# Two of 18 weight slots handed over at step 2 instead of step 4, and the later steps' order of work from step 2 on

## What is computed

```python
x = x + pool_mixer(rms_norm(x, norm_mix), pool_w, pool_scale)
h = rms_norm(x, norm_ffn)
# router: best of 4 groups, best 2 of its 8 experts, gates
for e in range(32):          # rows h[tokens of e]
    g, u = split(h_e @ w_gu[e])        # 1024 -> 2 x 512
    y_e = (silu(g) * u) @ w_dn[e]      # 512 -> 1024
x = x + sum over a token's two experts of gate * y_e
out = rms_norm(x, norm_final)
```

## Time and profile before

| | |
|---|---|
| median of 3 runs | 662.24 us (662.08 to 662.79) |
| the profiled execution | 663.27 us, of which the span is 661.5 us |
| PE, PE weight loads, DVE, ACT, POOL busy | 94%, 80%, 92%, 81%, 24% of the span |
| moved by DMA | 242.83 MB, mean 367 GB/s |
| PE's mean granted clock | 0.983 of full speed |

### The profile page before, as it was taken

One profiled execution on the slowest core, in us unless ns is written; L12 is line 12 of the kernel. 1 busy time (PEld: TensorE's weight loads), 2 busy tenths in 40 slices (PEclk: granted clock), 3 DMA queues, 4 the chain that ended last, 5 costly groups with the idle time before them and its releaser, 6 DMA issues.

```text
span 661.5 us, 9555 instructions
## 1 busy us (share of the span) xinstructions
PE 622.6 (94%) x3460; PEld 526.4 (80%) x3460; DVE 606.2 (92%) x501; ACT 535.7 (81%) x458; POOL 157.9 (24%) x127
## 2 busy tenths in 40 slices
PE   6899989999999999999999999897999989989983
PEld 4799978887888888888888888686877868767872
DVE  5887688989999999999999999897989889998987
ACT  5996626688898989898988988887879688978794
POOL 5000010032222222222222222252225222340311
PEclk9999989999999999999999999999999989989997
DMA  8997769999999999999999999999999999999985
GB/s 293 421 418 278 244 209 374 397 343 302 322 381 404 390 400 393 386 401 374 402 367 401 364 401 366 402 379 392 381 384 386 385 413 384 410 409 400 380 335 211
DMA packets 43637, 242.83 MB, mean 367 GB/s; under 512 B 8184, under 2 KB 9344, under 8 KB 19011
## 3 DMA queue, kind: packets, MB, share of 16 engines
q1 hardware_dynamic: 34322, 220.39, 84.2%
q0 software_dynamic: 9264, 21.79, 12.1%
HBM read 227.19 MB, written 26.21 MB: 383 GB/s over the span
## 4 chain that ended last, share of the span: by engine, by line
DMA 54%; PE 34%; DVE 5%; ACT 3%; issue 2%; SPq 0%; POOL 0%; ACTq 0%; POOLq 0%; DVEq 0%
DMA raw<-in_expert_w_gu 32%; PE psum L1724 19%; DMA raw<-in_expert_w_down 17%; PE psum L1736 3%; PE psum L1652 3%; PE psum L1670 2%; DMA total<-ysb,src_all 2%; PE psum L1638 2%; DMA raw<-total 1%; PE psum L1776 1%; DMA pw_in<-in_pool_w 1%; PE psum L1661 1%; DVE raw L1548 1%; PE psum L1678 1%; PE psum L1787 1%
## 5 line engine op out<-in xcount | busy, mean ns | idle before, releaser
L1210 DVE TENSOR_TENSOR w_lo<-raw,w_hi 128x2048 fp32r<-128x2048 f32 x113 | 255.4, 2284 | 7.8 <-ACT w_hi L884 7.4
L884 ACT ACTIVATE w_hi<-raw 128x2048 fp32r<-128x2048 f32 x113 | 213.5, 1914 | 21.8 <-DMA raw<-in_expert_w_gu 12.8
L1210 DVE TENSOR_TENSOR w_lo<-raw,w_lo 128x2048 fp32r<-128x2048 f32 x79 | 178.5, 2283 | 2.4 <-ACT w_lo L884 2.3
L884 ACT ACTIVATE w_lo<-raw 128x2048 fp32r<-128x2048 f32 x79 | 149.5, 1914 | 13.2 <-DMA raw<-in_expert_w_gu 10.2
L710 POOL DMA_INDIRECT total<-ysb,src_all x28 | 53.5, 1910 | 338.5 <-ACT ysb L979 323.9
L1724 PE MATMUL psum<-w_lo,x_hi 128*128 128x512 f32 x432 | 127.1, 397 | 5.8 <-DVE x_lo L1446 5.8
L1724 PE MATMUL psum<-w_lo,h_hi 128*128 128x512 f32 x376 | 108.3, 395 | 0.5 <-DVE h_lo L1480 0.5
L1724 PEld LDWEIGHTS psum<-w_lo,x_hi 128*128 128x128 f32 x432 | 81.0, 190 | 23.2 <-DVE x_lo L1446 6.7
L696 POOL DMA_INDIRECT xg<-normed,src_all x31 | 78.2, 2523 | 21.5 <-DVE src_all L1305 12.3
L1724 PEld LDWEIGHTS psum<-w_lo,h_hi 128*128 128x128 f32 x376 | 70.9, 190 | 15.5 <-DVE h_lo L1480 0.9
L1736 PE MATMUL psum<-w_lo,x_hi 128*128 128x512 f32 x276 | 74.0, 392 | 0.0
(11 more groups left out here) (208 smaller groups left out, 865.4 us busy)
## 6 DMA issues: line engine op xcount, KB each, us to landing
raw<-in_expert_w_gu SPq DMA_DIRECT2D x128, 1024.0 KB, 10.9
raw<-in_expert_w_down SPq DMA_DIRECT2D x64, 1024.0 KB, 11.8
res<-in_x SPq DMA_DIRECT2D x8, 512.0 KB, 9.7
normed<-nx POOLq DMA_DIRECT2D x8, 512.0 KB, 7.3
total<-res SPq DMA_DIRECT2D x8, 512.0 KB, 8.7
raw<-total SPq DMA_DIRECT2D x8, 512.0 KB, 13.4
out<-raw SPq DMA_DIRECT2D x8, 512.0 KB, 3.9
pw_in<-in_pool_w SPq DMA_DIRECT2D x1, 1024.0 KB, 8.1
```

Of the source, the lines that this page charges most:

```text
L884: nc.scalar.activation(hi_at(s0, j), raw[q][:], ACT.Copy).then_inc(hi_done, 1)
L1210: V.tensor_tensor(w_lo[q][:], raw[q][:], hi_at(s0, j).bitcast(f32), ALU.subtract)\
```

## The change

`FREE_STEP` goes from 4 to 2 and `FIRST` with it from 22 to 10: two raw slots become places for upper parts at pair 10, steps 2 and 3 use the later order on ACT and DVE, and two calls are moved so that they still happen in step 2. The slots 16 and 17 are never loaded; load m waits for pair m-16 from load 16 on. From pair 34 to pair 131 all that loads and upper parts wait for is as before.

```diff
-    FREE_STEP = HEAD
-    GIVEN = {HEAD: 2, E - 10: 2}
+    FREE_STEP = 2
+    GIVEN = {FREE_STEP: 2, E - 10: 2}
@@ ACT, step
                 if s < E - 1:
-                    copy_y(gate_all[:, s - 2:s - 1], start(s), s - 2)
+                    gates_of_y(s - 2)
+                    copy_y(gate_now[:] if s == 2 else gate_all[:, s - 2:s - 1], start(s), None if s == 2 else s - 2)
@@ DVE, early_step
                     if s == 1 and j == GU_PAIRS + 1:
                         turned_tables()
-                    if s == 2 and j == 0:
-                        tables_by_step()
@@ DVE, step
                     hidden(s - 1)
                     if s < E:
                         low_x(s, is_small(s))
+                    if s == 2:
+                        tables_by_step()
                 up_to(low_next, low_pair, s, n + 3)
```

## The result

| | before | changed |
|---|---|---|
| median of 12 runs | 662.60 us | 664.23 us |
| ratio, 95% interval | | 1.0019 (1.0011 to 1.0028) |
| the profiled execution, its span | 663.27, 661.5 us | 663.85, 662.1 us |
| PE, DVE, ACT busy | 94%, 92%, 81% | 94%, 91%, 81% |
| moved by DMA | 242.83 MB | 242.83 MB |

The change makes the kernel some 1.3 us slower. That is 0.19%, just inside the 0.2% taken as the bound of "no change", though the interval leaves 1 out. Two timings of one and the same kernel, further down, came out 0.28% apart, so the profiles have to carry the argument.

The account below looks back on a forecast made before the run. Free slots were taken to limit loads until about 220 us, then the DMA engines. Late start +0.8 us (between +1.9 and -0.3, PE's gain) on a median of 662.24 us gave 663.0 us; own range 661.6 to 664.1, overall to 665.3.

Parts of the forecast that it names:

- What bounds the kernel: Weight loads: limited by free slots up to about 220 us, after that by the DMA engines themselves.
- a shift that arises after 270 us: Stated sign of being wrong: the loads' shift arising in the DMA-limited part instead of before it.
- The lag at load 25: Load 25, waiting for pair 9, lands at 137.7 instead of 132.9 us: 4.8 us late.
- The hole behind load 33: Gap of 8 us between issues of loads 33 and 34, DMA partly idle; forecast to disappear.
- What makes the lag good: DMA idle time, 154 to 170 us, absorbs the late start: +1.9 us left by shares, -0.3 by bytes; +0.8 taken.
- The new stall: PE waits about 0.85 us for hid(1) near 129.5 us, as pairs 10 and 11 come first on ACT and DVE.
- The old one: PE's stall before the turn of hid(3) at 165.38 us, worth 1.15 us, was to go.
- The sum on PE: Old stall's 1.15 us less new stall's 0.85 us: PE gains 0.3 us from pair 21 on.
- Pair 130: Loads 142 and 143 wait for pairs two later; nothing expected, since SyncE waits for landings there; uncovered 2.7 us.
- The late start is not made good: Rival: idle share at 154 to 162 us can't be filled; +3.4 us, 665.6 us; chance 0.22.
- No stall: Rival: PE's stall near 129.5 us doesn't show and the stream isn't behind; -1.15 us, 661.1 us; chance 0.09.
- The clock falls: Rival: PE's clock drops to half rate at the stall near 129.5 us; +2.2 us, 664.4 us; chance 0.06.

Follow-up runs that it names:

- e5_wait_14: Kernel before, with loads 16 to 33 also waiting on SyncE for pair m-14, two pairs later than pair m-16; ratio 1.0086.
- e4_step4_head: Kernel before, but at the head of step 4 ACT takes one pair instead of two before silu(3), DVE none before hid(3); ratio 0.9978.
- e1_wait: Kernel before with one SyncE wait added: loads 16 to 33 also wait for pair m-16; compute orders unchanged; ratio 1.0013.
- e9_before_itself: Kernel before, letter for letter, timed against itself with no edit; ratio 0.9993.
- e3_hid_first: Changed kernel, but in step 2 silu(1) and hid(1) come before pairs 10 and 11 on ACT and DVE; ratio to before 0.9999.
- e2: Changed kernel's slots and places, but steps 2 and 3 in the early order, as in the kernel before; ratio to before 1.0019.
- e7: Changed kernel's slots and places with steps 2 and 3 in the early order, a repeat timing of e2; ratio to before 1.0005.
- e8: Kernel before, with loads 142 and 143 waiting for pairs 128 and 129 instead of 126 and 127; ratio 1.0017.
- e10: Same code as e8, timed again: kernel before with loads 142 and 143 waiting for the later pairs; ratio 0.9989.

## Why the prediction was right, point by point

The number fell inside the range and the sign was right, but in part by luck: the lag was made good in full, and then a loss that no term of the sum had brought the time back.

**What bounds the kernel** was right as to who waits for whom. e5_wait_14 moves the end by 0.86% with nothing but SyncE's waits. e4_step4_head lets PE run 1.1 us earlier, and the delay at load 181 is -0.8 us. The rule that I drew from it was wrong: that the end moves by as much as the stream is ahead or behind when it stops waiting for slots, a state "settled between 100 and 220 us". At load 52 the changed kernel is 0.4 us early and e1_wait on time; at load 181 they are 1.4 and 1.9 us late. The prediction had named the sign itself, a shift that arises after 270 us. Of the changed kernel's 1.4 us, 0.5 were there at load 74, near 270 us, and 0.9 came later.

**The lag at load 25**: forecast 4.8 us, measured 4.9. That close a match is luck, since the same load took 7.4 us to land in the kernel before and 5.9 us in e9_before_itself, which is the same code. The hole behind load 33 closed, the share from 154 to 170 us went to 1, and from load 34 on the waits are as before, each as forecast.

**What makes the lag good** was the weak term. I had two ends, +1.9 and -0.3 us, and took +0.8. The changed kernel's delay is 1.4 and 1.9 us in two profiles, e1_wait's 1.9. That looks like the upper end, the one by shares, but the way there was another. By shares 2.9 us of idle time could be filled, and 4.9 - 2.9 = 2.0 us had to stay; yet some 90 us after pair 0 nothing was left, which is the lower end. The count stopped at 170 us too early. From 170 to 177 us the changed kernel moved 352 GB/s against 327, and from 177 to 200 us 392 against 375, at shares of 1.02 against 0.98 and 1.00. And a share near 1 was indeed no full stream: the first 20 us of e5_wait_14 ran at 237 GB/s with a share of 0.66, which is 359 GB/s for a full share, where the kernel before moved 422 at 1.01. What stands in the place of the rest that "had to stay" is the loss after 250 us, which the sum had at nothing.

**The new stall**: forecast 0.85 us, measured 0.80 us idle, and pair 9 used 0.8 us late against pair 0. **The old one**: forecast 1.15 us, measured 1.12. The sum on PE was forecast as a gain of 0.3 us and is 0.4. But PE's balance of the two stalls, 1.15 - 0.85, does not give the end. Without the new stall, in e3_hid_first, pair 21 is used another 0.85 us earlier and the delay is 0.9 us smaller; in e2 and e7, without it and with a smaller gain on PE, the delay is 1.1 us smaller or more. That the new stall matters is shown, the path from it to the end is not.

**Pair 130**: forecast nothing. Two profiles show nothing; the two timings disagree with each other and can't show 0.1%.

**The rivals.** "The late start is not made good" gave +3.4 us and did not come: 154 to 162 us did fill, to 386 GB/s. "No stall" did not come; the stall stood where it was put. "The clock falls": the granted clock stayed at 1.00 over the 0.80 us gap, as it had over the 0.84 us one.

**The number**: 663.0 us forecast, 664.23 us measured in a comparison whose kernel before came to 662.60 us. By the ratio the shift is 1.3 us (0.7 to 1.9), forecast 0.8. It is close because two errors stood against each other: the lag vanished where 0.8 us of it were to stay, and the later loss had no term.

## What to carry to other kernels

Where a stream of loads is first limited by free buffers and then by the DMA engines, a late start of a few loads can be made good in the first part, and by more than the idle share says: count bytes from one early event, not busy shares alone. Don't take the state at the change-over for the end. Follow one load by its number up to the last, since here the delay came up behind it. And before buffers are traded for freedom of order, look whether the stall can be had out by order alone, as in e4_step4_head.

## What was not expected of the hardware, or of the measurement

Loads of 1 MB ran at 422 GB/s from 104 to 124 us in the kernel before, and at 357 GB/s from 124 to 154 us at a share of 0.99. The lower rate came again in every variant, with 331 GB/s at a share of 0.93 in the changed kernel and 342 GB/s in e1_wait, which had less queued. What makes it slower there stays open; no run was made for it. The same holds for the stretch from some 250 to 300 us, where a share of 1.01 to 1.02 moved 397 to 399 GB/s in some kernels and 379 to 393 in others.

The timings of one and the same code differed by more than their intervals suggest: 1.0017 and 0.9989 for e8 and e10, each with some 0.12 to 0.15% to either side. For effects of 0.1% the times of single events in a profile, counted from one early event, told more than a dozen timed runs: in the five kernels that leave PE's early work alone (e1, e5, e8, e9, e10), pair 21 came within 0.04 us of its place.
